# Weighing and adding the lower expert rows on GpSimd during the last expert pass

## What is computed

```
logits = h @ w_router                      # 512 x 8
top_logit, top_idx = top_k(logits, 2)
gates = softmax(top_logit)                 # two weights per token
y_e = (silu(h_e @ w_gate[e]) * (h_e @ w_up[e])) @ w_down[e]   # the rows h_e of expert e's tokens
out[token] = x[token] + gate_1 * y_e1[token] + gate_2 * y_e2[token]
```

## Time and profile before

| | |
|---|---|
| median of three runs | 1975.85 us |
| lowest and highest run | 1975.79, 1977.67 us |
| span of the profiled execution | 1974.2 us |
| TensorE matmul | 1929.4 us busy, 98% |
| VectorE | 749.4 us busy, 38% |
| ScalarE | 653.4 us busy, 33% |
| GpSimd | 497.9 us busy, 25% |
| mean granted TensorE clock | 0.996 |

### The profile page before, as it was taken

One profiled execution on the slowest core, in us unless ns is written; L12 is line 12 of the kernel. 1 busy time (PEld: TensorE's weight loads), 2 busy tenths in 40 slices (PEclk: granted clock), 3 DMA queues, 4 the chain that ended last, 5 costly groups with the idle time before them and its releaser, 6 DMA issues.

```text
span 1974.2 us, 28753 instructions
## 1 busy us (share of the span) xinstructions
PE 1929.4 (98%) x11831; PEld 1701.6 (86%) x11831; DVE 749.4 (38%) x1096; ACT 653.4 (33%) x1071; POOL 497.9 (25%) x265
## 2 busy tenths in 40 slices
PE   7999999999999999999899999999999999999996
PEld 7888878888888887876679999999999999888885
DVE  5655663200000007856641000010100102999996
ACT  4333223332222224367630001000010002888783
POOL 4547664355445544442111000000000000000010
PEclk9999999999999999999999999999999999999998
DMA  7962322233233232220019868788887887999995
GB/s 252 312 210 65 86 75 96 75 118 96 86 107 96 92 108 86 86 86 33 22 40 373 310 228 310 274 295 307 288 314 272 300 292 281 388 382 387 365 413 208
DMA packets 295103, 405.38 MB, mean 205 GB/s; under 512 B 11272, under 2 KB 211034, under 8 KB 294970
## 3 DMA queue, kind: packets, MB, share of 16 engines
q1 hardware_dynamic: 292666, 395.12, 57.3%
q0 software_dynamic: 2304, 8.39, 1.1%
HBM read 372.67 MB, written 30.80 MB: 204 GB/s over the span
## 4 chain that ended last, share of the span: by engine, by line
PE 93%; issue 3%; DVE 1%; POOL 1%; ACT 1%; SPq 0%; DVEq 0%; DMA 0%; ACTq 0%; POOLq 0%
PE ps L2059 21%; PE ps L2066 10%; PE ps L404 6%; PE ps L405 6%; PE ps L406 6%; PE ps L2120 5%; PE ps L2122 5%; PE ps L2121 5%; PE ps L422 3%; PE ps L423 3%; PE ps L424 3%; PE ps L552 2%; PE ps L554 2%; PE ps L553 2%; PE ps L439 1%
## 5 line engine op out<-in xcount | busy, mean ns | idle before, releaser
L1258 POOL TENSOR_TENSOR w_lo<-raw,w_hi 128x1024 fp32r<-128x1024 f32 (+1 forms) x159 | 387.9, 2450 | 346.5 <-ACT w_hi L951 346.5
L1906 DVE TENSOR_TENSOR s_lo<-s_raw,s_hi 128x1024 fp32r<-128x1024 f32 x198 | 235.3, 1222 | 22.1 <-ACT s_hi L2266 13.6
L2508 DVE TENSOR_TENSOR hid<-ps,silu_g 128x160 f32<-128x160 f32 x110 | 35.7, 324 | 543.0 <-ACT silu_g L2241 543.0
L2241 ACT ACTIVATE silu_g<-ps 128x160 f32<-128x160 f32 x110 | 33.5, 304 | 585.8 <-PE ps L2059 585.8
L951 ACT ACTIVATE w_hi<-raw 128x1024 fp32r<-128x1024 f32 (+1 forms) x159 | 164.8, 1044 | 187.9 <-PE ps L424 112.7
L2059 PE MATMUL ps<-xT,w_gate 128*128 128x132 f32 (+1 forms) x1760 | 224.2, 281 | 0.0
L2059 PE MATMUL ps<-xT,w_up 128*128 128x132 f32 (+1 forms) x1760 | 224.2, 281 | 0.0
L404 PE MATMUL ps<-act_a_hi,w_hi 128*128 128x512 f32 x568 | 221.4, 390 | 0.0
L406 PE MATMUL ps<-act_a_hi,w_lo 128*128 128x512 f32 x568 | 221.0, 389 | 0.0
L405 PE MATMUL ps<-act_a_lo,w_hi 128*128 128x512 f32 x568 | 221.0, 389 | 0.0
L2266 ACT ACTIVATE s_hi<-s_raw 128x1024 fp32r<-128x1024 f32 x198 | 205.6, 1059 | 42.7 <-PE ps L2122 37.3
(11 more groups left out here) (395 smaller groups left out, 2914.0 us busy)
## 6 DMA issues: line engine op xcount, KB each, us to landing
w_gate<-in_moe_w_gate SPq DMA_DIRECT2D x55, 1024.0 KB, 5.3
w_up<-in_moe_w_up SPq DMA_DIRECT2D x55, 1024.0 KB, 7.6
w_down<-in_moe_w_down SPq DMA_DIRECT2D x55, 1024.0 KB, 10.2
s_raw<-in_moe_w_gate SPq DMA_DIRECT2D x33, 1024.0 KB, 7.5
s_raw<-in_moe_w_up SPq DMA_DIRECT2D x33, 1024.0 KB, 7.4
s_raw<-in_moe_w_down SPq DMA_DIRECT2D x33, 1024.0 KB, 7.3
raw<-in_even_w_in SPq DMA_DIRECT2D x43, 512.0 KB, 5.2
raw<-in_attn_w_qkv SPq DMA_DIRECT2D x24, 512.0 KB, 3.7
```

Source lines behind the costliest of these rows:

```text
L1258: pool.tensor_tensor(w_lo[:, u % HL_SLOTS, 0:size(u)], raw[:, u % RAW_SLOTS, 0:size(u)], flat(w_hi[:, u % HL_SLOTS, 0:size(u)]), ALU.subtr ...
L1906: return eng.tensor_tensor(s_lo[u % S_HL][:], s_raw[u // 2 % S_RAW][:, u % 2, :], s_hi[u % S_HL][:].bitcast(F32), ALU.subtract)
```

## The change

VectorE no longer adds the lower rows. GpSimd does it instead, behind the lower gathers and ahead of its wait for the last store. It waits for the gates (`gates_made`) and for all four gathers, which share one semaphore (`lower_back`). It multiplies each tile of `y_lower` by its gate, in place, with the gate's column broadcast over 1024 columns; a drain; it adds each tile to `x_sb`. These are four multiplies and four adds of 128 x 1024. VectorE then waits, for each tile, for `lower_added` and for the higher gather, and does one `scalar_tensor_tensor`. The four lower ones and the drain are gone.

```diff
--- before.py
+++ after.py
@@ -1866,7 +1866,8 @@
     tile_done, silu_done, hid_made = sem("tile_done"), sem("silu_done"), sem("hid_made")
     down_done, acc_read = sem("down_done"), sem("acc_read")
     y_turned, y_copied, y_stored = sem("y_turned"), sem("y_copied"), sem("y_stored")
-    y_back = [sem(f"y_back{i}") for i in range(2 * NT)]
+    lower_back, higher_back = sem("lower_back"), [sem(f"higher_back{i}") for i in range(NT)]
+    gates_made, lower_added = sem("gates_made"), sem("lower_added")
     places_ready, pick_made, picked = sem("places_ready"), sem("pick_made"), sem("picked")
     xT_started = sem("xT_started")
     out_made, out_stored = sem("out_made"), sem("out_stored")
@@ -2357,21 +2358,28 @@
         pool.wait_ge(extras_made, 1)
         n = n_extra(pool)
 
-        def gather(dst, k):
+        def gather(dst, k, back):
             for tt in range(NT):
                 j = NT * k + tt
                 pool.indirect_dma_start(dst[:, tt, :], None, y_dram,
                                         bass.IndirectOffsetOnAxis(ap=slot_i[:, j:j + 1], axis=0)
-                                        ).then_inc(y_back[j], 16)
+                                        ).then_inc(back(tt), 16)
 
 
         pool.wait_ge(s_y_stored, 16 * (SMALL - 1))
         pool.wait_ge(y_stored, n * 32 + 32 * WIDE)
         pool.sem_inc(pool_step, 1)
-        gather(y_lower, 0)
+        gather(y_lower, 0, lambda tt: lower_back)
+        pool.wait_ge(gates_made, 1)
+        pool.wait_ge(lower_back, 16 * NT)
+        for tt in range(NT):
+            pool.tensor_tensor(y_lower[:, tt, :], y_lower[:, tt, :], gate[:, tt:tt + 1].to_broadcast([P, D]), ALU.mult)
+        pool.drain()
+        for tt in range(NT):
+            pool.tensor_tensor(x_sb[:, tt, :], x_sb[:, tt, :], y_lower[:, tt, :], ALU.add).then_inc(lower_added, 1)
         pool.wait_ge(s_y_stored, 16 * SMALL)
         pool.sem_inc(pool_step, 1)
-        gather(y_higher, 1)
+        gather(y_higher, 1, lambda tt: higher_back[tt])
 
     @block.vector
     def _(dve):
@@ -2502,7 +2510,8 @@
                 dve.tensor_tensor(part, g, flags, ALU.mult)
         dve.drain()
         for k in range(2):
-            dve.tensor_tensor(gate[:, 4 * k:4 * k + 4], work[:, 8 * k:8 * k + 4], work[:, 8 * k + 4:8 * k + 8], ALU.add)
+            ins = dve.tensor_tensor(gate[:, 4 * k:4 * k + 4], work[:, 8 * k:8 * k + 4], work[:, 8 * k + 4:8 * k + 8], ALU.add)
+        ins.then_inc(gates_made, 1)
 
         def weigh_up(f, bank):
             dve.tensor_tensor(hid[:, f, :], ps[:, bank, CAP:2 * CAP], silu_g[:, f % 2, :], ALU.mult
@@ -2617,16 +2626,11 @@
                 dve.wait_ge(down_done, x * ROUNDS + (WIDE + 1) * ROUNDS)
                 copy_acc()
 
-        for k, got in enumerate((y_lower, y_higher)):
-            for tt in range(NT):
-                j = NT * k + tt
-                dve.wait_ge(y_back[j], 16)
-                if tt == 0:
-                    dve.drain()
-                ins = dve.scalar_tensor_tensor(x_sb[:, tt, :], got[:, tt, :], gate[:, j:j + 1], x_sb[:, tt, :],
-                                               ALU.mult, ALU.add)
-                if k:
-                    ins.then_inc(out_made, 1)
+        for tt in range(NT):
+            dve.wait_ge(lower_added, tt + 1)
+            dve.wait_ge(higher_back[tt], 16)
+            dve.scalar_tensor_tensor(x_sb[:, tt, :], y_higher[:, tt, :], gate[:, NT + tt:NT + tt + 1], x_sb[:, tt, :],
+                                     ALU.mult, ALU.add).then_inc(out_made, 1)
 
     block.__exit__(None, None, None)
```

## The result

The changed kernel is slower: 1986.72 us in the median (1985.92 to 1989.49, five runs) against 1977.67 us for the kernel before, run beside it (1975.79 to 1978.66). The ratio is 1.0049, 95% interval 1.0038 to 1.0059. The forecast was 6.45 us more, 1982.3 in a range of 1979 to 1987. The medians differ by 9.05 us, and the ratio makes it 9.7: the direction is right, and the estimate of the difference is 2.6 to 3.3 us short. The forecast counted from 1975.85 us; the five runs beside the change have 1977.67, so 1.8 us of the distance between 1982.3 and 1986.72 lie in this base. From the forecast's own base the change comes to 1984.9 us, above the forecast's narrower range of 1979.5 to 1984.3.

What follows compares the result with a forecast made beforehand. TensorE, busy 98% of the span, was taken as the bound, with VectorE close behind. Starved TensorE adds 7.1 us and the tail takes off 0.65: 1975.85 + 6.45 = 1982.3 us, range 1979.0 to 1987.0.

Steps and rivals of the forecast that it cites:

- the mechanism and its place: Last expert pass, about 1891.9 to 1915.7: each of eight GpSimd instructions holds up one VectorE low part, starving TensorE 7.1 us.
- The PSUM-reading instructions: Last pass: two VectorE instructions reading PSUM can run beside GpSimd, taking 1.2 us off the loss.
- The lead: Last pass, chunk 3: low parts are ready 3.8 us before TensorE begins their unit (other bound 4.2), absorbing that much.
- Part 2: Eight GpSimd instructions inside the last pass: 17.2 us alone, free on GpSimd, but 7.1 us of starved TensorE.
- the size of the holds: Last pass: VectorE loses 1.5 us per GpSimd multiply and 2.0 per add, 14.0 us in all (11.6 to 17.2).
- the free time of VectorE: Last pass: VectorE's idle time, 1.3 us per 16.8 us round, covers 1.9 us of the loss over a 23.8 us stretch.
- the tail: After the last matmul: four adds leave VectorE, which then follows the higher gathers; gain 0.65 us (0 to 1.3).
- The exclusion rule: Skill page, read literally: two-SBUF-input VectorE and SBUF-reading GpSimd instructions exclude each other throughout, a loss of 17.2 us.
- The clock rival: Last pass: starved TensorE is granted 1.2 GHz, 2 us per stretch, two of them 4: 1984.3 to 1986.3; chance 0.10.
- Held too little to matter: Last pass: free time, PSUM instructions and lead, 6.9 us, cover all holds; only the tail speaks, 1975.2 us; chance 0.13.
- Longer holds: Last pass: holds last the whole GpSimd duration, or multiplies equal adds; lag 9.1 to 10.9, time 1984.3 to 1986.1; chance 0.17.

Runs made afterwards that it cites:

- e1: The changed kernel without its eight GpSimd multiplies and adds; gathers, waits and shortened VectorE end stay: pass 69.56 us, ratio 1.0001 to the kernel before.
- e2: The changed kernel with sixteen GpSimd memsets of 128x1024 in place of the eight multiplies and adds: pass 69.57 us, ratio 1.0004 to the kernel before.
- e5: The changed kernel with lower adds back on VectorE, three in its idle time ahead of the last row copy, one behind: ratio 1.0002 to the kernel before.
- e8: The changed kernel with GpSimd's multiplies as tensor_scalar, the gate a per-partition scalar: pass 75.22 us, ratio 1.0029 to the kernel before.
- e4: The changed kernel with each of the eight GpSimd instructions waiting for five more weight units on TensorE: pass 78.72 us, ratio 1.0052 to the kernel before.

## Why the prediction was right and wrong

**Right: the mechanism and its place.** Each of the eight instructions keeps VectorE from a low part, one by one, through a stretch that began at 1892.5 and ended at 1918.0 (forecast 1891.9 and 1915.7, in an execution that started 1.38 us quicker). e1 and e2 confirm the reason: without arithmetic, or with writes alone, the cost is nil. The PSUM-reading instructions ran beside GpSimd as forecast: the low parts behind L2556 and L2576 lost 1.1 and 1.6 us instead of 1.7 and 2.2, together the 1.2 us of the forecast. The lead was nearly right. The last held low part is that of gate unit 2 in chunk 3. Before, it was ready at 1904.80 and its weight load ran at 1908.88, 4.1 us later; after, it was ready at 1919.08 and the load ran at 1919.14. So 4.0 us of lead were used up (forecast 3.8, with 4.2 as the other bound). Part 2's statement that the work is free on GpSimd holds, too: the first of the higher gathers starts 4.88 us after the last copy, and before it was 4.81.

**Wrong: the size of the holds, 1.6 us in all.** This is the term of 14.0 us, 4 x 1.5 + 4 x 2.0. A held low part takes 2.91 us beside a multiply and 3.40 beside an add, against 1.22: holds of 1.7 and 2.2 us, 15.6 for the eight. With 1.2 us less for the PSUM-reading instructions that is 14.4, and the rows agree: VectorE stood for 1.35 us beside the first multiply, and its low parts lost 12.9 (7.15 - 3.5 = 3.65, 10.11 - 4.6 = 5.5 and 12.94 - 9.16 = 3.8, where three, four and eight take 3.5, 4.6 and 9.16 us when they run back to back in the changed kernel's later rounds). I had taken 0.4 us off GpSimd's own 1.91 and 2.40 us; what comes off is 0.2. Why it is less here than in the early layers isn't shown.

**Wrong: the free time of VectorE, 0.5 us.** I had 1.9 us, a share of the stretch as it would be after the change, 23.8 us. But idle time belongs to the old schedule. The low parts made in that stretch took 12.9 us before (1891.9 to 1904.8). Back to back they start 1.13 us apart (eight in 9.16 us in the later rounds of the changed kernel), and the two PSUM-reading instructions among them take 0.6 each, so these eleven need 11.5 us. Idle time was 1.4 us: the 0.72 ahead of 1892.64 and 0.7 behind it. More of it came later in the old round (1.2 us within the eight of the earlier trace rows, behind the second of them), where it could cover nothing.

Together: 15.6 - 1.2 - 1.4 - 4.0 = 9.0 us, against 14.0 - 1.9 - 1.2 - 3.8 = 7.1. That is the pass's 9.01.

**Wrong: the tail, 0.65 us.** I let the later gathers keep their 5.4 us and put the effect of earlier stores only into the bound. Measured: -0.08 to the end of the last add, and +0.31 to the end of the span. Besides the changed kernel, the eight others of the table with this tail and free stores lie between 19.36 and 20.40 us, seven of them above the one profile of before, 19.60. The last add ends 15.9 us after the copy in the mean of the ten profiles with this tail, as before (15.93), and the slowest higher gather lands after 5.5 to 6.3 us in them, where I had left it at 5.4. e5's interval reaches 1.4 us to the faster side, so the medians alone can't rule out a gain of 0.65; the profiles give none. Whether the tail loses some tenths isn't shown, as there is one profile of before.

**The exclusion rule.** The page "SBUF — State Buffer" of the Trainium skill (section "Who interferes with whom") says that a VectorE instruction with two SBUF inputs contends with a GpSimd instruction that reads SBUF, and not with one that only writes it. e2 agrees: sixteen memsets cost nothing. It calls the sharing an exclusive lock; its words "for the whole instruction" stand beside VectorE's 2-port modes, and the prediction applied them to two inputs. The tensor_tensor here nearly meets them, 1.7 of 1.89 us and 2.2 of 2.36, and the tensor_scalar of e8 doesn't, 0.7 of 4.2. There the measurement decides.

**The rivals.** The clock rival didn't occur in the pass of the changed kernel's profile, and did in e4. "Held too little to matter" is refuted by the rows. "Longer holds" had the time about right (a lag of 9.1 us with multiplies at 2.0 us), and half of its mechanism: the holds are longer than I took, by 0.2 us each, but neither is the multiply as slow as the add nor is a hold the whole duration.

**Open.** What makes the tensor_scalar 4.2 us long and its holds short isn't shown; it was never run here with VectorE idle. Nor is it shown why the clock fell in e4 and not in the changed kernel, which has longer idle time in all.

## What to carry to other kernels

Before moving work to GpSimd, look at what VectorE runs beside it: where those instructions have two SBUF inputs and VectorE is over 90% busy for TensorE (15.45 of 16.8 us here), each GpSimd tensor_tensor takes nearly its own length from VectorE, and TensorE pays it once the lead of a few buffers is gone (8 instructions, 9.0 us; 4, 3.4; the same 8 beside a VectorE that was 5% busy with PSUM-reading work, nothing). When you count free time against an added hold, count the idle time inside the old work that the hold covers, not a share of the new, longer stretch. At an end that is full of DMA traffic (90% here) shorter arithmetic gave back nothing that the profiles or the medians show.

## What the runs showed of the hardware

- GpSimd memsets (15 us beside the low parts, e2) don't hold VectorE instructions with two SBUF inputs; GpSimd tensor_tensor does, by 1.7 us (one operand broadcast) or 2.2 us (two full operands) per instruction of 128x1024. VectorE instructions with one input in PSUM keep their 0.68 us beside it.
- GpSimd's tensor_scalar of 128x1024 float32 with a per-partition scalar took 4.2 us beside a busy VectorE, longer than a tensor_tensor with the same factor broadcast (2.8 there, 1.89 alone), and held VectorE for 0.7 us.
- TensorE's granted clock stayed at 1.00 through the 16.9 us from 1902.3 in which it was busy 57%, with weight loads standing for up to 2.2 us (after), and fell to 0.50 for some 3 us in e4 behind waits of 1.06 and 2.15 us, with matmuls of 128x256 between them.
- The same code is granted 1.2 GHz for 3.4 us in some executions and not in others: near 21 us in nine of the thirteen profiled ones, and near 932 or 988 us in four. Each time the rest of the kernel comes 1.2 to 1.8 us later.
